# Gate and up of both feed-forward stages: the first two hidden blocks add A12 B21 in the bank of A11 B11, and gate's A22 and GpSimd's start are placed anew

## What is computed

```
hn = rms_norm(h, ffn_pre_g)                                  # first block
ff = (jax.nn.silu(hn @ w_gate) * (hn @ w_up)) @ w_down
h = h + rms_norm(ff, ffn_post_g)
...
h = _rmsnorm(x, norm_ffn[l])                                 # second block
gate, up = jnp.split(h @ w_gu[l], 2, axis=-1)
x = x + (jax.nn.silu(gate) * up) @ w_down[l]
```

## Time and profile before

| | us |
|---|---|
| median of 3 runs | 2384.74 (2384.32 to 2384.88) |
| the profiled execution's own time | 2383.25 |
| its span in the profile | 2381.4 |
| TensorE busy | 2310.8 |
| VectorE busy | 1434.8 |
| ScalarE busy | 962.7 |
| GpSimd busy | 874.0 |

### The profile page before, as it was taken

The page is one execution under the profiler, slowest core; times in us unless marked ns, Lnnn a source line. Parts: engine busy times, 40 slices in busy tenths (PEclk is TensorE's granted clock), DMA queues, the critical chain, the costliest instruction groups (busy, mean ns, idle before and its releaser), DMA issues.

```text
span 2381.4 us, 30526 instructions
## 1 busy us (share of the span) xinstructions
PE 2310.8 (97%) x11502; PEld 1940.3 (81%) x11502; DVE 1434.8 (60%) x2283; ACT 962.7 (40%) x1941; POOL 874.0 (37%) x733
## 2 busy tenths in 40 slices
PE   7999999999999999999999999999989999999998
PEld 5887888788888888888998877888868888888887
DVE  6999924845354577784634766253584545357776
ACT  4126544432323245454634645134353232324543
POOL 3000125287787700032113121121329778780002
PEclk9999999999999999999999999999999999999999
DMA  5121124243333368654002100141424233336865
GB/s 154 47 66 63 63 89 129 66 133 97 102 115 102 117 245 288 220 198 102 19 18 73 42 5 19 54 149 64 130 75 131 86 115 104 113 115 233 278 217 196
DMA packets 217141, 275.84 MB, mean 116 GB/s; under 512 B 16987, under 2 KB 144700, under 8 KB 214178
## 3 DMA queue, kind: packets, MB, share of 16 engines
q1 hardware_dynamic: 199442, 210.57, 28.6%
q10 hardware_dynamic: 17552, 63.31, 6.8%
HBM read 205.27 MB, written 68.57 MB: 115 GB/s over the span
## 4 chain that ended last, share of the span: by engine, by line
PE 85%; DVE 8%; ACT 2%; DMA 2%; issue 2%; POOL 1%; SPq 1%; DVEq 0%; POOLq 0%; ACTq 0%
PE P L489 25%; PE P L491 25%; PE P L490 25%; PE P L2799 3%; PE P L2776 2%; PE P L2787 2%; PE P L501 1%; DMA h<-ht 1%; DVE s L1568 1%; ACT p L2852 1%; PE P L1365 0%; DVE al L519 0%; DVE wl L2361 0%; POOL ws L2638 0%; PE P L1391 0%
## 5 line engine op out<-in xcount | busy, mean ns | idle before, releaser
L489 PE MATMUL P<-ah,wh 128*128 128x512 f32 x1120 | 440.4, 393 | 2.4 <-DVE al L519 2.3
L490 PE MATMUL P<-al,wh 128*128 128x512 f32 x1120 | 437.6, 391 | 0.0
L491 PE MATMUL P<-ah,wl 128*128 128x512 f32 x1120 | 437.5, 391 | 0.0
L489 PE MATMUL P<-wh,ah 128*128 128x512 f32 (+2 forms) x1128 | 425.4, 377 | 0.0
L491 PE MATMUL P<-wh,al 128*128 128x512 f32 (+2 forms) x1128 | 423.3, 375 | 0.0
L490 PE MATMUL P<-wl,ah 128*128 128x512 f32 (+2 forms) x1128 | 423.0, 375 | 0.0
L571 POOL TENSOR_TENSOR stats<-stats,epsc 128x1 f32<-128x1 f32 x86 | 35.7, 416 | 814.6 <-ACT xn L1818 420.9
L489 PEld LDWEIGHTS P<-ah,wh 128*128 128x128 f32 x1120 | 211.4, 189 | 46.5 <-DVE al L519 2.5
L491 PEld LDWEIGHTS P<-ah,wl 128*128 128x128 f32 x1120 | 211.3, 189 | 44.4
L490 PEld LDWEIGHTS P<-al,wh 128*128 128x128 f32 x1120 | 211.5, 189 | 43.4
L491 PEld LDWEIGHTS P<-wh,al 128*128 128x128 f32 x1128 | 212.2, 188 | 37.1
(11 more groups left out here) (336 smaller groups left out, 4280.5 us busy)
## 6 DMA issues: line engine op xcount, KB each, us to landing
rf<-ff_rows SPq DMA_DIRECT2D x154, 256.0 KB, 5.1
stage<-in_w_down_dram SPq DMA_DIRECT2D x110, 256.0 KB, 3.8
ff_rows<-sb ACTq DMA_DIRECT2D x22, 1024.0 KB, 5.0
stage<-in_w_gu_dram SPq DMA_DIRECT2D x44, 512.0 KB, 5.1
h<-ht ACTq DMA_DIRECT2D x24, 512.0 KB, 5.0
xr<-h SPq DMA_DIRECT2D x24, 512.0 KB, 5.0
stage<-in_w_in_dram SPq DMA_DIRECT2D x22, 512.0 KB, 3.9
stage<-in_w_gate_dram SPq DMA_DIRECT2D x22, 512.0 KB, 4.0
```

The costliest lines, as they stand in the source:

```text
L489: e.matmul(out, lh, rh, start=start, stop=False, skip_group_check=onto)
L490: e.matmul(out, lh, rl, start=False, stop=False, skip_group_check=onto)
L491: return e.matmul(out, ll, rh, start=False, stop=stop, skip_group_check=onto)
```

## The change

C11 of the first pair is no longer summed by VectorE: A12 B21 of m = 0 and 1 goes, without clearing, to the bank that holds A11 B11 (bank 5 and 6), once ScalarE has copied that out. The two copies move up in ScalarE's queue, the first ahead of T2's second high half, the second behind it. Silu reads C11 of m = 0 from PSUM, and VectorE's product reads C11 of m = 1 from there. The two `first_sum` are gone from VectorE's queue. VectorE lowers A22 of m = 0 before the first evacuations (ScalarE makes its high half sooner to match), takes the sum of S1 for m = 0 sooner, and makes T4 in two parts. GpSimd gets a wait for the last low half of T4 in front of m = 2.

```diff
         def freed(self, m, op):
             if op == "A11":
-                return (ev, (name, m, "U2")) if m < 2 else (ev, (name, m, "F11")) if m % 2 else (gl, (name, m, "C11"))
-            return ev, (name, m, {"S2": "U2", "S3": "C21", "S1": "C12", "A12": "C11"}[op])
+                return (ev, (name, m, "F11")) if m % 2 else (gl, (name, m, "C11"))
+            return ev, (name, m, {"S2": "U2", "S3": "C21", "S1": "C12"}[op])
...
         def product(self, m, op):
-            b = {"A11": x, "A12": x if m >= 2 else y, "S2": y, "S3": z, "A22": z, "S1": w, "S4": w}[op]
-            begins = op in ("A11", "S2", "S3", "S1") or (op == "A12" and m < 2)
+            b = {"A11": x, "A12": x, "S2": y, "S3": z, "A22": z, "S1": w, "S4": w}[op]
+            begins = op in ("A11", "S2", "S3", "S1")
             if begins:
                 claim(b, *self.freed(m, op))
+            elif op == "A12" and m < 2:
+                PE.wait_ge(cp, (self.name, m, "A11"))
...
         def silu(self, m, b):
-            if b == "C11" and m >= 2:
+            if b == "C11":
                 src = P[:, self.banks(m)[0], :]
                 AC.wait_ge(mm, (self.name, (m, "A12")))
-                AC.wait_ge(ev, (self.name, m - 1, "F11"))
+                if m >= 2:
+                    AC.wait_ge(ev, (self.name, m - 1, "F11"))
...
             T.upper_act("T1", 1)
+            AC.wait_ge(l_h[0], (T.name, 6))
+            self.copy(0)
             T.upper_act("T2", 1)
+            self.copy(1)
             T.late_act(2)
             T.upper_act("T2", 2)
             T.late_act(3)
             T.upper_act("T2", 3)
-            AC.wait_ge(l_h[0], (T.name, 6))
-            self.copy(0)
-            self.copy(1)
...
-            for op in ("S1", "S4", "A22"):
-                for m in range(2):
-                    self.upper(UNIT_AT[m, op])
+            for m, op in ((0, "S1"), (1, "S1"), (0, "A22"), (0, "S4"), (1, "S4"), (1, "A22")):
+                self.upper(UNIT_AT[m, op])
...
         def dve(self):
-            for u in range(3):
+            for u in range(4):
                 T.lower_dve("T2", u)
-            DV.wait_ge(sq, (T.name, "h", NT - 1))
-            stored(DV, T.name)
-            self.first_sum(0)
-            T.lower_dve("T2", 3)
             self.lower_dve(1, "S2")
-            self.first_sum(1)
...
             self.lower_dve(1, "S1")
+            self.lower_dve(0, "A22")
             self.last_early_sum()
+            DV.wait_ge(sq, (T.name, "h", NT - 1))
+            stored(DV, T.name)
             self.sums(0, "S2")
             self.sums(1, "S2")
             self.sums(0, "S3")
-            for u in range(4):
-                T.fourth_dve(u)
+            T.fourth_dve(0)
+            T.fourth_dve(1)
             self.sums(1, "S3")
+            self.sums(0, "S1")
             self.lower_dve(0, "S4")
-            self.sums(0, "S1")
+            T.fourth_dve(2)
+            T.fourth_dve(3)
             self.lower_dve(1, "S4")
             self.sums(1, "S1")
             for u in range(4):
                 T.lower_dve("T4", u)
-            self.lower_dve(0, "A22")
             self.lower_dve(1, "A22")
...
             T.squares_pool(6)
             T.squares_pool(7)
+            PL.wait_ge(al, (T.name, "T4", 3, "low"))
             for m in range(2, NF):
```

More of the change, by code:

```diff
@@ L2372, in products_dve @@
         def products_dve(self):
[L2374 to L2381, removed]
+            for b in ("C22", "C11"):
+                c = self.block(1, b)
+                if b == "C11":
+                    DV.wait_ge(mm, (self.name, (1, "A12")))
+                else:
+                    DV.wait_ge(ev, (self.name, 1, b))
+                DV.wait_ge(gl, (self.name, 0, b))
+                DV.e.tensor_tensor(c, P[:, self.banks(1)[0], :] if b == "C11" else c, self.block(0, b), ALU.mult).then_inc(
+                    *ev.up((self.name, 1, "F" + b[1:])))
         def sums(self, m, op):
@@ L2422, in sums @@
                     times("C12", c12)
[L2424 to L2428, removed]
         def dve(self):
```

## The result

| | before | after |
|---|---|---|
| median, us | 2384.53 (2382.84 to 2384.88, 4 runs) | 2372.19 (2369.63 to 2372.44, 4 runs) |
| ratio to before | | 0.9947 (95%: 0.993 to 0.9964) |
| the profiled execution's own time | 2383.25 | 2369.63 |
| wait on GpSimd before S2 of m = 2, first / second stage | 2.62 / 3.41 | 0 / 0 |
| wait on T2, first / second | 2.42 / 2.34 | 1.74 / 1.77 |

The kernel is 12.3 us faster, where 9.8 were forecast. The waits went as forecast within 0.1 us, but for T2's in the first stage, 1.74 us where 2.1 were forecast; the gain is 2.5 us larger than the sum.

What follows compares the result with a forecast made beforehand. TensorE, busy 2310.8 of 2381.4 us, was taken as the bound. First stage 3.7 plus second 6.4 made 10.1 us, less 0.3 for row sums: 2384.74 - 9.8 = 2374.9 us, range 2372.0 to 2379.0 (forecast's own 2372.5 to 2377.5).

Steps and rivals of the forecast that it cites:

- T2's and T3's waits: TensorE before S2 and S3 of m = 0: together 0.9 us gained in the first stage, 1.2 in the second.
- GpSimd's wait: TensorE before S2 of m = 2: the whole wait goes, 2.8 us in the first stage, 3.5 in the second.
- The margin: GpSimd's weights for S2 of m = 2: there at 466.0, wanted at 468.0, so 2.0 us left over.
- My bound: Before S2 of m = 2: six GpSimd operations at 1.74 us need 10.4 us, and 0.5 us of wait stays.
- First stage in all: First feed-forward stage: 0.9 us at T2 and T3 plus 2.8 at GpSimd's wait, 3.7 us gained.
- Second stage, waits: Second feed-forward stage: 1.2 us gained at T2 and T3, 3.5 at GpSimd's wait with its restart.
- Row sums: VectorE's four before C22 of m = 2, beside GpSimd: S4 waits 0.15 us a stage, 0.3 taken off.
- Rival A: VectorE's row sums each wait out a GpSimd operation, four take 7.9 us; 2377.4 us, chance 0.05.
- The clock: Behind S2 of m = 2, second stage: no lower clock without the wait, 1.7 us gained, 0 to 1.7 possible.
- B: Before S2 of m = 2: GpSimd still last, 1 to 2 us of each wait stay; 2378 to 2380, chance 0.09.
- C: Loads released by something else than A22 of m = 0; only T2 and T3 gain, 2382.6 us, chance 0.07.
- D: ScalarE's queue stalls at the copy until tile 6 is stored; 2390 us at 14 to 15 us, chance 0.03.

Runs made afterwards that it cites:

- e6: The kernel before once more, all switches of the change off; 2383.82 us, ratio 1.0003 to the kernel before.
- e1: The whole change in the first feed-forward stage only, the second as in the kernel before; ratio 0.9989 to the kernel before.
- e2: The whole change in the second feed-forward stage only, the first as in the kernel before; ratio 0.9973 to the kernel before.
- e5: The changed kernel once more, nothing altered; 2371.99 us, ratio 0.995 to the kernel before.
- e10: The changed kernel a third time, nothing altered; 2372.99 us, ratio 0.9952 to the kernel before.
- e15: The changed kernel again, nothing altered; 2371.87 us, ratio 0.9952 to the kernel before.
- e8: The changed kernel with GpSimd's work on m = 2 held until TensorE's A22 of m = 0, both stages; 2380.08 us.
- e13: The changed kernel with GpSimd held after lowering A11 of m = 2 until TensorE's A22 of m = 1, both stages; 2383.07 us.
- e9: The changed kernel with T2 of the first three tiles lowered by GpSimd instead of VectorE; 2371.77 us, ratio 0.9946 to the kernel before.
- the adds alone: Against the kernel before, only the addition in the bank, copies moved up and two sums gone, both stages; ratio 0.9996.
- e14: As e9, but GpSimd first waits for VectorE's norm of the last tile; 2370.82 us, ratio 0.9948 to the kernel before.

## Where the forecast held, and the step that failed

- **T2's and T3's waits**: 2.1 and 1.7 forecast for T2, 1.74 and 1.77 found; 0.3 each for T3, 0.32 and 0.30 found. A12 of m = 0 did begin late in the first stage, by 0.2 us where 0.3 were forecast, and the trace names ScalarE's copy for it. The delay went on to VectorE, as forecast. Before, 3.98 us lay between the start of the last tile's norm and the step that makes its T2 (433.21); after, it is 4.15, with 0.28 us idle for ScalarE's half. The norm before; then TensorE's weight load (PEld) for A12, the norm and that step after:

```profile
429.23 1.28 DVE L710 SCALAR_TENSOR_TENSOR xn<-ht,stats,gb 128x1024 f32<-128x1024 f32 x1
```

```profile
426.18 0.19 PEld L489 LDWEIGHTS P<-ah,wh 128*128 128x128 f32 x1 [0.21 <-ACT go L2196]
...
426.60 1.28 DVE L710 SCALAR_TENSOR_TENSOR xn<-ht,stats,gb 128x1024 f32<-128x1024 f32 x1
...
430.75 0.69 DVE L829 TENSOR_TENSOR t4s<-P,als 128x512 f32<-128x512 f32 x1 [0.28 <-ACT ah L817]
```

  S2 of m = 0 starts 7.99 us behind this norm for 8.41 before: 0.4 sooner, the 0.6 less 0.2. So the step held, and the 2.1 was a slip: when TensorE begins both A12 and S2 0.3 us later, the wait between them is 2.42 - 0.6 = 1.8.
- **GpSimd's wait**: gone in both stages. The margin was 0.7 us (465.21 less 463.06 and a third of 4.26), not 2.0. GpSimd's first step took 2.29 us beside VectorE, for 1.29, so the six operations needed 8.9 us, not 7.8. My bound (all six crowded) covered it.
- **First stage in all**: 3.7 forecast. From a point 40 matmuls ahead of A12, so that its late start counts, to S4 of m = 2, it went from 63.95 to 60.15 (mean of the four traces of after): 3.8.
- **Second stage, waits**: 4.7 forecast (1.2 and 3.5). Before's stretch without what the lower clock took is 59.44 - (15.36 - 13.77) = 57.85, with 15.36 and 13.77 from S2 to S4 of m = 2 in its second and first stage; the mean of the four traces of after is 52.69. That is 5.2. Most of what I missed stands in two rows of before, A22's last matmul and A11's first of m = 2:

```profile
1776.90 0.39 PE L491 MATMUL P<-t4x,wl 128*128 128x512 f32 x1
1777.35 0.50 PE L489 MATMUL P<-ah,wh 128*128 128x512 f32 x1
```

  Matmuls follow each other by 0.23 us there, these by 0.45, and the first one is 0.1 longer: some 0.3 us went before A11 as well, too short for the list of waits. I had read the list and not the row before the wait.
- **Row sums**: 0.3 us taken off. They did grow, 6.9 us from the first to C22 where they had taken 6.25, and S4 of m = 2 came 0.26 us late in the first stage of after, not at all in the second. But before's first stage had lost 0.17 there too. Net about nothing, so 0.3 us more gain. Rival A, full exclusion, priced them at 2.0 each; they took 1.67 to 1.87.
- **The clock, the step that failed**: its mechanism was right and its size was not. 1.7 us was taken, since the profiled execution showed a lower clock behind one wait of four on T2 and GpSimd, and the range let it fall to 0 but, within the two stages, not rise. Three traces hold a stage of before for each side. Behind the second GpSimd wait, S2 to S4 of m = 2 took 15.36, 16.51 and 16.40 (before, e6, e1), for 13.77 without it: 2.3 on average, not 1.6. Behind the first one 0, 1.5 and 0 (before, e6, e2), and behind T2's 0.4 once: 0.6 on average. Together **3.0, not 1.7** (2.32 and 0.64 before rounding). I had one execution, and took for its price what it happened to show. The mean granted clock of all executions on record says the same, and more strongly. In the groups of e5, e10 and e15 the kernel before has 0.9914, 0.9907 and 0.9908 (36 executions, e6's among them, then 11 and 17), the changed kernel 0.9940, 0.9937 and 0.9940 (6 each). Among the 89 executions of before in the four groups, compared within each group, a clock lower by 0.001 goes with a time longer by 1.2 us. By these figures the clock is worth 3.2 to 3.9 us of the gain (an estimate), and 1.7 is too little.
- **The sum with the measured terms**: 3.8 + 5.2 + 3.0 = 12.0 us. Measured are 12.3 in the first comparison, and by the ratios of e5, e10 and e15 11.9, 11.4 and 11.4. Clock 1.3, the second stage's waits 0.5, row sums 0.3 and the first stage 0.1 make up the 2.2 between 9.8 and 12.0.
- **The range**: the forecast's own ended at 2372.5, and was widened to 2372.0; the time came to 2372.19, below the first and at the very end of the second. B, C and D did not happen: the load started 0.8 us behind the start of A22's lowering, GpSimd was not last, and the store was never waited for.
- **How sure**: that a wait on GpSimd of this length brings the lower clock with it is shown by e8 and e13, which add nothing else, lost 3.1 and 3.5 us beyond the waits, and ran at a mean clock lower by 0.0019 and 0.0022. That the same surplus explains the change has two supports: the stretches of three executions of each stage, with an error of about 1 us, and the mean clocks of all executions. These last don't say in which part of the kernel the clock fell.

The Trainium skill, "SBUF — State Buffer", section "Who interferes with whom", calls the ports that VectorE and GpSimd share an exclusive lock, the rule that I had called half right. It says "for the whole instruction" only of VectorE's two-port modes, but by e9's row this holds for two SBUF operands as well, and better than I judged: 1.12 of 1.30 us were waited out, and the row sums' 1.77 is 0.68 and 1.09. I had compared 1.77 with 0.68 + 1.29 and taken the missing 0.2 for a sign against it.

## What to carry to other kernels

A wait of TensorE costs its length and, in the longer ones here, a stretch at the lower clock in many executions but not in all; price it from several traces, and shorten all such waits together, since taking one away may only lengthen the next, as the adds alone did. When VectorE's list sets a wait, count the steps between two due points before moving anything: what stands ahead of both moves both and changes no later wait. An idle GpSimd can take over low halves, if it is placed where VectorE's steps read PSUM and not SBUF twice; here it took 3.0 us out of the two stretches (e14), which the medians did not show.

## What the runs showed of the hardware that I had not expected

- In one execution, of two waits of 2.48 us in front of the same instructions, one had the lower clock behind it and the other had not (e8). Over all traces, counting the waits on GpSimd and on T2 in the two stages, it was 7 of 7 from 3.1 us on, 7 of 15 between 2.3 and 2.8, 0 of 18 at 1.7 to 1.8.
- A lower clock behind the wait on GpSimd made the way from S2 to S4 of m = 2 15.1 to 15.4 us (six times) or 16.4 to 16.6 us (three times) for 13.7 to 13.8: 1.3 to 1.6 or 2.7 to 2.8 us more, by the execution. Behind T2's wait it cost 0.4 us or nothing, because the waits behind it gave the rest back.
- VectorE's norm of 128x1024 grew from 1.28 to 2.40 us beside one step of GpSimd of 1.30, and GpSimd's lowering grew from 1.29 to 2.29 or 3.70 where it began beside VectorE's steps on SBUF, which kept their 0.6 us.
- The executions of before reach over 12 us, with a standard deviation of 3.0 (89 in the four groups), those of after over 6, with 1.5 (22): half of the spread went. It isn't tied to these waits alone, as e14, without them, has 3.0 again.
